# Two modulation blocks requested and summed ahead of x and its norm, two broadcast rows requested later

## What is computed

```
c_act = jax.nn.silu(c)
mod = (c_act @ ada_w[i] + ada_b[i])[:, None, :]
sh1, sc1, g1, sh2, sc2, g2 = jnp.split(mod, 6, axis=-1)
h = rmsnorm(x, mix_norm_pre[i]) * (1.0 + sc1) + sh1
...
qkv = h @ w_qkv
...
logits = jnp.where(mask, scores + bias, -1e30)      # 16 heads, window of 128 tokens
...
x = x + g1 * rmsnorm(y, mix_norm_post[i])
h = rmsnorm(x, ffn_norm_pre[i]) * (1.0 + sc2) + sh2
y = swiglu(h, ffn_w_in[i], ffn_w_out[i])
```

## Time and profile before

| | us |
|---|---|
| median of 3 runs | 2038.01 |
| lowest, highest | 2037.85, 2040.68 |
| the profiled execution | 2037.74 |
| its span | 2035.7 |
| mean granted PE clock, share of full | 0.972 |
| busy: PE, DVE, ACT, POOL | 1731.8, 1469.5, 920.2, 622.0 |

### The profile page before, as it was taken

One profiled execution on the slowest core, in us unless ns is written; L12 is line 12 of the kernel. 1 busy time (PEld: TensorE's weight loads), 2 busy tenths in 40 slices (PEclk: granted clock), 3 DMA queues, 4 the chain that ended last, 5 costly groups with the idle time before them and its releaser, 6 DMA issues.

```text
span 2035.7 us, 22044 instructions
## 1 busy us (share of the span) xinstructions
PE 1731.8 (85%) x6989; PEld 1021.4 (50%) x6989; DVE 1469.5 (72%) x3271; ACT 920.2 (45%) x2397; POOL 622.0 (31%) x575
## 2 busy tenths in 40 slices
PE   3979998999887899987777788998999877778776
PEld 3759997988765444432222223464555323223222
DVE  7787888898867678766676677446876776777675
ACT  3664444445643444544444445234544444444443
POOL 1540000000004354343334443114455434443431
PEclk7989998999998999999999998999999999999999
DMA  9666677777748999999999999659999999999996
GB/s 383 262 227 228 248 283 277 259 252 242 269 139 331 421 421 421 421 421 418 421 421 422 421 421 421 263 205 411 421 415 421 421 421 421 422 421 421 422 422 254
DMA packets 119404, 723.25 MB, mean 355 GB/s; under 512 B 12012, under 2 KB 13828, under 8 KB 43000
## 3 DMA queue, kind: packets, MB, share of 16 engines
q0 software_dynamic: 75152, 541.35, 64.2%
q1 hardware_dynamic: 44136, 180.50, 24.2%
HBM read 720.72 MB, written 1.08 MB: 355 GB/s over the span
## 4 chain that ended last, share of the span: by engine, by line
DMA 40%; PE 30%; DVE 17%; ACT 5%; issue 4%; POOL 3%; SPq 0%; DVEq 0%; ACTq 0%; POOLq 0%
DMA X<-in_k_uv,EI 23%; PE PS L2304 11%; DMA Z<-in_k_uv,EI 8%; DMA W<-in_k_uv,EI 5%; DVE junk L1977 4%; PE PS L1990 4%; PE PS L1992 3%; PE PS L1991 3%; PE PS L2280 3%; DVE HALF L1602 2%; POOL X L1107 2%; DVE WL L1614 2%; DMA HALF<-in_k_ada 2%; DMA W<-in_k_ada 1%; PE PS L2321 1%
## 5 line engine op out<-in xcount | busy, mean ns | idle before, releaser
L2304 PE MATMUL PS<-X,dg 128*128 128x512 f32 x1380 | 665.4, 615 | 127.9 <-ACT dg L1116 127.2
L1977 DVE CUSTOM_DVE_ANT_0 junk<-H,X 128x1024 f32<-128x1024 f32 x345 | 422.0, 1223 | 238.6 <-DMA X<-in_k_uv,EI 226.7
L1107 POOL DMA_INDIRECT X<-in_k_uv,EI x345 | 368.2, 1067 | 512.7 <-PE PS L2304 360.2
L2304 PEld LDWEIGHTS PS<-X,dg 128*128 128x128 f32 x1380 | 248.5, 193 | 503.3 <-ACT dg L1116 288.4
L1116 ACT ACTIVATE CF<-DOT 128x1 f32<-128x1 f32 x512 | 103.8, 203 | 658.3 <-DVE DOT L1977 653.3
L2304 PE MATMUL PS<-Z,dg 128*128 128x512 f32 x480 | 233.7, 613 | 59.4 <-ACT dg L1116 58.9
L1977 DVE CUSTOM_DVE_ANT_0 junk<-H,Z 128x1024 f32<-128x1024 f32 x120 | 146.8, 1223 | 95.4 <-DMA Z<-in_k_uv,EI 92.2
L1116 ACT ACTIVATE dg<-CP,CG 128x128 f32<-128x128 f32 x512 | 205.7, 402 | 17.9 <-PE PS L2304 1.2
L1990 PE MATMUL PS<-XH,WH 128*128 128x256 f32 x592 | 174.2, 294 | 13.3 <-DVE WL L1614 12.0
L2304 PEld LDWEIGHTS PS<-Z,dg 128*128 128x128 f32 x480 | 83.7, 189 | 191.5 <-ACT dg L1116 124.7
L1991 PE MATMUL PS<-XL,WH 128*128 128x256 f32 x592 | 170.4, 288 | 0.0
(11 more groups left out here) (320 smaller groups left out, 2589.1 us busy)
## 6 DMA issues: line engine op xcount, KB each, us to landing
HALF<-in_k_ada SPq DMA_DIRECT2D x66, 512.0 KB, 5.2
W<-in_k_ada SPq DMA_DIRECT2D x24, 1024.0 KB, 7.0
Y<-in_k_ada SPq DMA_DIRECT2D x15, 1024.0 KB, 7.2
W<-in_k_win SPq DMA_DIRECT2D x15, 1024.0 KB, 8.4
W<-in_k_ffi SPq DMA_DIRECT2D x13, 1024.0 KB, 6.7
Y<-in_k_ffi SPq DMA_DIRECT2D x9, 1024.0 KB, 5.6
W<-in_ffn_w_out SPq DMA_DIRECT2D x8, 1024.0 KB, 5.1
W<-in_peer_wq SPq DMA_DIRECT2D x8, 1024.0 KB, 19.5
```

Source lines behind the costliest of these rows:

```text
L1107: e.indirect_dma_start(out=WS[k][:, :], out_offset=None, in_=I[f"k_uv{ly}"][:, :], in_offset=bass.IndirectOffsetOnAxis(ap=EI[t][:, j:j + 1 ...
L1977: e.tensor_tensor_reduce(junk, H[:, t, :], d[:, 0:D], 1.0, 0.0, ALU.mult, ALU.add, DOT[:, j:j + 1]).then_inc(v_dot, 1)
L2304: p = e.matmul(PS[:, 2 * t + q, :], dgb[n % 4][:, :], d[:, D + q * 512:D + (q + 1) * 512], start=(j == 0), stop=(j == 127))
```

## The change

In the opening SP's requests come in another order: c, block 0, block 1, x, block 2, `CP`, block 3, block 4, and then the short vectors. The sums of blocks 0 and 1 stand ahead of `rms` and `normed`, and `small1` stands right behind these and the seven `xp`. The requests for c_2 and c_ctx_2 move from POOL, behind `BE`, to SP, in turn n = 12 of the attention loop.

```
-    P("rms", 0)
-    P("normed", 0)
-    for c in range(8):
-        if c < 7:
-            P("xp", 0, c, first[c])
-    after = {0: "small1", 2: "bias", 3: "small2"}
+    P("lda", 0)
+    P("lda", 1)
+    P("ldx")
+    P("lda", 2)
+    P("ldcp")
+    P("lda", 3)
+    P("lda", 4)
+    after = {1: "small1", 2: "bias", 3: "small2"}
     for m in range(6):
         ada(m, 0)
         ada(m, 1)
+        if m == 1:
+            P("rms", 0)
+            P("normed", 0)
+            for c in range(7):
+                P("xp", 0, c, first[c])
         if m in after:
             P(after[m])
...
         if n < 16:
             P("as", n)
+        if n == 12:
+            P("ldc2")
...
+                elif kind == "ldc2":
+                    w.wait_ge(d_td, 16)
+                    e.dma_start(CB[1], spread(I["c_2"][0:1, :])).then_inc(d_c2, 16)
+                    e.dma_start(CB[2], spread(I["c_ctx_2"].rearrange("(a b) -> a b", a=1))).then_inc(d_c2, 16)
...
                     e.dma_start(BE[:, :, :], bass.AP(tab_d, 0, [[1, 128], [512, 16], [1, 384]])).then_inc(d_be, 16)
-                    e.dma_start(CB[1], spread(I["c_2"][0:1, :])).then_inc(d_c2, 16)
-                    e.dma_start(CB[2], spread(I["c_ctx_2"].rearrange("(a b) -> a b", a=1))).then_inc(d_c2, 16)
```

More of the change, by code:

```diff
@@ L64, in ada @@
             P("ldh", m, j)
-        elif j == 0:
+        elif j == 0 and m > 4:
             P("lda", m)
@@ L957, in _ @@
                     e.dma_start(CB[0], spread(I["c"][0:1, :])).then_inc(d_c, 16)
+                elif kind == "ldx":
                     e.dma_start(XS[:, :, :], I["x"].rearrange("b (t p) d -> p (b t) d", p=128)).then_inc(d_x, 16)
+                elif kind == "ldcp":
                     e.dma_start(CP[:, :], I["k_cp"]).then_inc(d_cp, 16)
+                elif kind == "ldc2":
+                    w.wait_ge(d_td, 16)
+                    e.dma_start(CB[1], spread(I["c_2"][0:1, :])).then_inc(d_c2, 16)
+                    e.dma_start(CB[2], spread(I["c_ctx_2"].rearrange("(a b) -> a b", a=1))).then_inc(d_c2, 16)
                 elif kind == "small1":
```

## The result

| | before | after |
|---|---|---|
| median of 20 runs each, us | 2039.83 | 2042.34 |
| the profiled execution | 2037.74 | 2041.16 |
| its span | 2035.7 | 2039.4 |
| ratio after / before, with its 95% interval | | 1.0013 [1.0007, 1.0019] |

The change costs 2.65 us (1.4 to 3.9): less than the 0.2% that a measurement tells from no change by itself, but with 20 runs of each the interval lies wholly above 1. Forecast were +2.6 us and 2040.6 (2037.0 to 2043.5); the median of before over 20 runs lies 1.8 above that of the three shown ahead of the prediction, so the difference is what is to be compared.

What follows compares the result with a forecast made beforehand. DVE was taken to set the opening's pace, with SP's full queue setting it for DVE up to block 2. +5.7 - 1.4 - 1.7 = +2.6 us on the median 2038.01 gave 2040.6, range 2037.0 to 2043.5.

Steps and rivals of the forecast that it cites:

- Term one: Opening: DVE's copy of the short vectors waits for them and PE's transposes, so block 2 starts late: +5.7 us.
- the upper bound: Opening delay at most +6.5 us, if transposes run at PE's lower clock or the vectors' landing takes 2.0 us.
- The second need: Opening: the copy also needs PE's 14 transposes, which wait for `H` and `CP` (18.2) and take 3.13 us.
- The rival that let them come early: Opening: vectors not held by the blocks ahead, delay +3.7 us, +0.6 in all: 2038.6; chance 0.2.
- Terms two and three: Attention: PE's wait for block 11 before its third scores vanishes (-1.36 us), and the slow clock behind it (-1.7).
- term three: Attention: without PE's wait before its third scores the clock stays at full level: -1.7 us.
- The time that I gave block 11: Attention: block 11, requested at 60.7, takes about 6 us and lands at 66.7, in time.
- Part three: Moving the c_2 and c_ctx_2 requests from POOL to SP is worth nothing of its own and costs nothing.
- The change as meant: Rival: the copy does not hold DVE in the opening, block 11 lands earlier: -3.4 us, 2034.6; chance 0.07.
- Nothing given back: Rival: in the attention block 11 again takes 11.8 us, so the opening's +5.7 us stays: 2043.7; chance 0.17.
- The signs named: Trace signs: DVE idle about 6 us before block 2, no idle for `BE` or block 11, unit 4 2.5 us late.

Runs made afterwards that it cites:

- vectors_late: The kernel before with SP's request for the short vectors moved from behind block 0 to behind block 4; 2045.61 us, ratio 1.0033.
- before_again: The kernel before run once more, with no change; 2039.28 us, ratio 1.0002.
- c2_only: The kernel before with only c_2 and c_ctx_2 moved from POOL to SP in turn 12; ratios 0.9993 and, repeated, 0.9990.
- opening_only: The kernel after with c_2 and c_ctx_2 back on POOL behind `BE`; three times, ratios 1.0026, 1.0021 and 1.0016.
- all_late: The kernel after with short-vector transpose and copy behind block 5's sums, bias table's sum behind block 3's, later vectors' copies behind block 4's; ratio 0.9993.
- copy_late: The kernel after with PE's transpose and DVE's copy of the short vectors moved behind block 5's sums; 2040.06 us, ratio 1.0003.
- vectors_behind_block0: The kernel after with only SP's request for the short vectors moved back behind block 0's; 2041.96 us, ratio 1.0008.
- block11_later: The kernel before with block 11's two sums on DVE moved two turns later in the attention; 2038.95 us, ratio 0.9998.

## Why the prediction was right, and where it was not

**Term one: right in its mechanism, 0.9 us short.** The sum had +5.7, measured were +6.63 (24.71 against 18.08). Block 0, x, the norm and the transposes came within 0.5 us of what was said (8.30, 14.72, 18.1, 18.61 to 21.8). What was mis-sized is the time of the vectors from the byte count to the landing: their last byte was due at 22.1, and I added the 1.0 us of block 2. They took 2.0, as block 0 does in the earlier trace rows; I had this only in the upper bound. SP's queue in after, from 21 to 22, 22 to 23 and 23 to 24 us:

```profile
q1 hardware_dynamic: 106, 0.41, 100.0%
...
q1 hardware_dynamic: 132, 0.40, 105.2%
...
q1 hardware_dynamic: 48, 0.39, 100.7%
```

At like bytes the many packets are the short ones, and they were still being moved between 22 and 23. So up to one of the two microseconds was spent in the queue, after the count said that it had moved as many bytes as stood ahead, and not in landing.

That short vectors queue behind megabytes was a reading of the earlier trace rows; vectors_late shows it directly, with 8.5 us. The Trainium skill (DMA: Bandwidth & Descriptors, "Queues, rings and completion order") says that on each engine descriptors are taken in ring order; by that rule the vectors wait, and the trace agrees (they landed at 24.1 behind block 4, and by 22.1 when they were asked for behind block 0). The rival that let them come early is out.

The second need, PE's 14 transposes, was as priced (3.22 us). What I missed is that the bias table's sum needs them too. It cost nothing in the changed kernel, since the copy had waited longer, but it would have spoiled the obvious mend.

**Terms two and three: the right sum from the wrong terms.** I had -1.36 for PE's wait before the third scores and -1.7 for the slow clock behind it, -3.1 together; measured from the first scores to unit 5's were -2.85 (6.81 to 3.96). But before_again has the same wait with the clock at 1.00, and gains 0.4 where term three had 1.7. What sets the pace from 66.5 to 79 us is DVE: in before_again it has no idle time there, in before only 0.32 us ahead of unit 5. From block 11's first sum to unit 5's bias addition it takes 12.37 to 12.39 us in eight traces (both c2_only, all three opening_only, all_late, vectors_late, before_again), 12.51 or 12.52 in four (both of after, copy_late, vectors_behind_block0; in after 0.13 of it is a wait for the scores of unit 1), and 12.76 in the first trace of before, the one with the slow clock there. So what counts is when that sum starts, and so the account is:
- first scores: +6.81;
- unit 0's addition on DVE: 69.91 against 63.92, +5.99, because it no longer waits for `BE` behind the scores (-0.82);
- block 11's sums: 71.00 against 66.80, +4.20, because DVE's wait of 1.71 us for the block is gone (-1.79);
- unit 5's addition: +3.96 (-0.24, the clock and the rest).

The step that failed is the pricing of both terms on PE, under the condition that they "count only as far as PE sets the pace": PE did not. The stretch of slow clock went from 68.43 to past 72.22 on PE, but it was mostly time that PE would have spent waiting. That the sum came out within 0.3 us is luck. In block11_later, where DVE had got ahead, the same kind of stretch did hold it up, by 1.73 us. The time that I gave block 11, 6 us, was 7.1: requested at 61.78, landed at 68.9, 2.1 us before DVE's sum. The waits of DVE for `BE` and block 11 stood in the earlier trace rows and I read them as what releases PE, not as slack of the engine that sets the pace.

**Part three: not shown to be right.** I had c_2's move at nothing, since the wait for block 11 was gone anyway. It isn't gone without the move: opening_only has it again, with 0.71 to 1.90 us on DVE, though little is left of that at unit 5. In the old opening the move takes 0.95 us off block 11's transfer and is the only part of the change found to pay.

**The rivals.** The change as meant (-3.4) needs not only the copy out of the way but the bias table too; all_late, which does both, comes to 0.9993 [0.9984, 1.0003], no more than c2_only alone. The opening's new order gains nothing by itself: the same bytes through the same full queue. "Nothing given back" did not happen here (block 11 landed in time), but nearly does in vectors_late. Two sums about the rivals were wrong. DVE releases PE 1.66 us after block 11 lands (66.77 to 68.43), so with a request at 60.7 and PE ready at 72.8 that rival would have begun at a landing time of 10.4 us, not 9.6. And -3.4 us lies within the 4.1 that count as no change, so the chance of the change as meant belonged there and not to faster.

**The end.** The span grew by 3.7 us in the profiled executions, the mean by 2.7. The signs named came out: DVE idle for 6.39 us, the transpose at 24.1 (said: about 23), no idle time for `BE` or block 11. The first product came at 43.4 (said: 42 to 43), the clock was at 1.00 from 50 and not from 46, and unit 4 was 3.5 us late and not 2.5, the 0.9 us of term one. A delay at 80 us does reach the end, less what scatters: about +4.1 at 290 us for after against the mean of before's two traces, +2.7 at the end; -1.2 and -1.5 for c2_only; +7.5 and +5.7 (+-2.2) for vectors_late. The forecast of +2.6 is thus nearer to the end's value than its steps deserve.

## What to carry to other kernels

When a transfer is put earlier on a full queue, list every step that is pushed behind it on each in-order engine, and for each the slowest thing that it needs: a copy of 80 short rows, free before, held the engine that set the pace for 6.6 us, and a small table's sum, as free before, held it for 2.8 once the copy was out of the way. To price a wait that goes away, first find the engine that is without gaps behind it; a slow clock on another engine is worth little while that engine has waits to fill (here 0.4 us in place of 1.7), but reaches the others where it has none (1.73 us on DVE in block11_later). And compare single executions only up to the first place where two executions of one kernel part.

## What the runs showed of the hardware

- The granted clock at the start is not a property of the kernel. It was 1.00 up to 60 us in one execution of before and fell to 0.50 at 18 us, up to 42, in the other; opening_only had both kinds too. The first execution of before took 25.55 us from the first product to the first scores, the one at full clock 25.21, so it costs little there.
- A fall of the clock in the attention depends on the execution as well: with PE's wait of 1.36 it came (0.50 over 70 to 72), with 1.41 it did not (1.00).
- Five short vectors of 80 rows in all landed 2.0 us after their last byte was due by the queue's byte count, where block 2, 1 MiB on the same full queue, took 1.0. Their packets were still being moved up to a microsecond after that time (132 packets with 0.40 MB from 22 to 23 us in after, 48 with 0.39 from 23 to 24).
- Two executions of one kernel keep a distance that is constant to 0.02 us from 80 to 125 us. Behind that some stay together to the end (both of after), others part: those of opening_only stand up to 5.0 us apart at 400, after a fall of the clock and a stretch of full queue.
